# Hybrid decoder on one core: the two softmax maps of the prompt's attention are combined by ScalarE and GpSimd

## What is computed

```
s = jnp.einsum('bqhmd,bkhmd->bhmqk', qs, ks).astype(F32) * (DIFF_DH ** -0.5)
s = s + bias[None, :, None]
s = jnp.where(rel >= 0, s, jnp.finfo(F32).min)
p = jax.nn.softmax(s, axis=-1)
a = p[:, :, 0] - lam * p[:, :, 1]
return jnp.einsum('bhqk,bkhd->bqhd', a, v.astype(F32))
```

## Time and profile before

| What | Value |
|---|---|
| three runs, median (range) | 4095.96 us (4091.81 to 4100.94) |
| the profiled execution: its span | 4093.1 us; no time around it is listed |
| busy over the span: TensorE, VectorE, ScalarE, GpSimd | 90%, 45%, 28%, 3% |
| the prompt's attention, stretch 2322 to 3188 us | 866 us, 21% of the span |
| busy in that stretch: TensorE, VectorE, ScalarE, GpSimd | 757.94, 735.26, 571.56, 0 us |
| granted TensorE clock in that stretch | 0.96 of full speed |

### The profile page before, as it was taken

One profiled execution on the slowest core, in us unless ns is written; L12 is line 12 of the kernel. 1 busy time (PEld: TensorE's weight loads), 2 busy tenths in 40 slices (PEclk: granted clock), 3 DMA queues, 4 the chain that ended last, 5 costly groups with the idle time before them and its releaser, 6 DMA issues. The chain is left out here.

```text
span 4093.1 us, 57158 instructions
## 1 busy us (share of the span) xinstructions
PE 3702.2 (90%) x19551; PEld 3035.2 (74%) x19551; DVE 1841.7 (45%) x4144; ACT 1162.0 (28%) x1916; POOL 119.0 (3%) x156
## 2 busy tenths in 40 slices
PE   5999897995999989998999688888889799869999
PEld 4888796773888868887888577777777667458887
DVE  2222211555555531113222388888888222165554
ACT  2111111332222120102111266666666211121111
POOL 0000001110000000000000000000000000000000
PEclk9999998997999989999999899999999899879999
DMA  4211322336222231213212622222210546242221
GB/s 143 72 67 67 112 89 85 114 112 223 79 74 87 72 131 67 72 69 144 74 64 69 133 57 51 53 64 64 64 33 12 199 170 219 97 173 72 86 82 49
DMA packets 305344, 385.23 MB, mean 94 GB/s; under 512 B 153574, under 2 KB 211719, under 8 KB 305175
## 3 DMA queue, kind: packets, MB, share of 16 engines
q1 hardware_dynamic: 305174, 383.18, 28.9%
HBM read 278.63 MB, written 104.47 MB: 94 GB/s over the span
## 5 line engine op out<-in xcount | busy, mean ns | idle before, releaser
L234 PE MATMUL vg_ps_y<-vg_w_hi,vg_x_hi 128*128 128x512 f32 x1088 | 428.0, 393 | 10.9 <-ACT vg_w_hi L263 10.9
L236 PE MATMUL vg_ps_y<-vg_w_lo,vg_x_hi 128*128 128x512 f32 x1088 | 425.0, 391 | 0.0
L238 PE MATMUL vg_ps_y<-vg_w_hi,vg_x_lo 128*128 128x512 f32 x1088 | 424.8, 390 | 0.0
L1506 PE MATMUL att_ps_o<-att_v,att_a_t 128*128 128x128 f32 x2176 | 296.1, 285 | 51.0 <-ACT att_a_t L1567 50.6
L1506 PEld LDWEIGHTS att_ps_o<-att_v,att_a_t 128*128 128x128 f32 x2176 | 278.0, 197 | 76.0 <-ACT att_a_t L1567 53.2
L1634 DVE TENSOR_SCALAR_CACHE_REDUCE att_s<-att_ps_s,att_far 128x512 f32<-128x512 f32 (+3 forms) x608 | 326.6, 582 | 6.0 <-PE att_ps_s L1479 1.9
L1555 ACT ACTIVATE att_s<-att_s,att_neg 128x128 f32<-128x128 f32 (+15 forms) x256 | 307.2, 1200 | 2.7 <-DVE att_neg L1651 2.1
L1478 PE MATMUL att_ps_s<-att_k_hi,att_q_hl 128*128 128x512 f32 (+3 forms) x640 | 260.8, 414 | 11.7 <-DVE att_s L1634 10.8
L234 PEld LDWEIGHTS vg_ps_y<-vg_w_hi,vg_x_hi 128*128 128x128 f32 x1088 | 205.3, 189 | 53.3 <-issue 11.7
L238 PEld LDWEIGHTS vg_ps_y<-vg_w_hi,vg_x_lo 128*128 128x128 f32 x1088 | 205.2, 189 | 43.0
L236 PEld LDWEIGHTS vg_ps_y<-vg_w_lo,vg_x_hi 128*128 128x128 f32 x1088 | 205.3, 189 | 41.6
(11 more groups left out here) (269 smaller groups left out, 6431.2 us busy)
## 6 DMA issues: line engine op xcount, KB each, us to landing
smp_k_pg<-in_cache_k SPq DMA_DIRECT2D x64, 512.0 KB, 5.1
smp_v_pg<-in_cache_v SPq DMA_DIRECT2D x64, 512.0 KB
factors<-vg_out SPq DMA_DIRECT2D x68, 256.0 KB, 2.0
res_factors<-factors SPq DMA_DIRECT2D x34, 512.0 KB
res_o<-mixer_out SPq DMA_DIRECT2D x34, 512.0 KB, 4.4
att_k_nat<-out_k SPq DMA_DIRECT2D x128, 128.0 KB, 2.7
att_q_nat<-diff_q SPq DMA_DIRECT2D x128, 128.0 KB, 3.0
gla_x<-gla_qka SPq DMA_DIRECT2D x17, 520.0 KB, 3.4
```

Source lines behind the costliest of these rows:

```text
L234: nc.tensor.matmul(ps_y[g][:, 0:width[g]], x_hi[u][:, k, :], w_hi[:, k, cols], start=(k == 0), stop=False)
L236: nc.tensor.matmul(ps_y[g][:, 0:width[g]], x_hi[u][:, k, :], w_lo[:, k, cols], start=False, stop=False)
L238: mm = nc.tensor.matmul(ps_y[g][:, 0:width[g]], x_lo[u][:, k, :], w_hi[:, k, cols], start=False, stop=(k == KD - 1))
L1506: mm = nc.tensor.matmul(ps_o[:, 0:D_VD], a_t[n % 2][:, (b % 4) * P:(b % 4 + 1) * P], v_sb[u][:, b, :], start=(b == 0), stop=(b == i))
```

## The change

The pass over n columns leaves VectorE. The weight now has two buffers. ScalarE gets a new step `scale`, which multiplies the second map's exponentials in place by w, behind `high` and ahead of the next tile's `exps`. GpSimd gets a program for the phase: for each tile it waits for `p2_scaled` and for the buffer `a` to be turned, adds the two maps into `a`, and signals `a_done`. VectorE's `combine` ends with the weight.

```diff
-        weight = sb("weight", [P, 1])
+        weight = [sb(f"weight{i}", [P, 1]) for i in range(2)]
...
+                def scale(H, i):
+                    n = (i + 1) * P
+                    act.wait_ge(s["weight_done"], after(T * H + i + 1))
+                    nc.scalar.activation(s_sb[i % 2][:, 1, 0:n], s_sb[i % 2][:, 1, 0:n], ACT.Copy,
+                                         scale=weight[i % 2][:, 0:1]).then_inc(s["p2_scaled"], 1)
...
                             high(H + 1, 1 - u, slots(i)[1] + n, is_q, m, g)
                         more = not (last and i + 1 >= T)
+                        scale(H, i)
                         if more:
                             exps(*ahead(H, u, i, 1), 0)
...
-                    nc.vector.scalar_tensor_tensor(weight[:, :], total[i % 2][:, 0:1], core.neg_lambda[:, :],
+                    if not (isinstance(H, int) and H == 0 and i < 2):
+
+                        dve.wait_ge(s["p2_scaled"], after(T * H + i - 1))
+                    nc.vector.scalar_tensor_tensor(weight[i % 2][:, :], total[i % 2][:, 0:1], core.neg_lambda[:, :],
                                                    inv[i % 2][:, 1:2], ALU.mult, ALU.mult).then_inc(s["weight_done"], 1)
-                    dve.wait_ge(s["weight_done"], after(T * H + i + 1))
-
-                    dve.wait_ge(s["a_turned"], after(GROUPS * H + first_group[max(i - 1, 0)]))
-                    nc.vector.scalar_tensor_tensor(a[i % 2][:, 0:n], s_sb[i % 2][:, 1, 0:n], weight[:, :],
-                                                   s_sb[i % 2][:, 0, 0:n], ALU.mult, ALU.add).then_inc(s["a_done"], 1)
...
+            @block.gpsimd
+            def _(pool):
+                def head(H, u, last):
+                    for i in range(T):
+                        n = (i + 1) * P
+                        pool.wait_ge(s["p2_scaled"], after(T * H + i + 1))
+                        stand_alone(pool, core)
+
+                        pool.wait_ge(s["a_turned"], after(GROUPS * H + first_group[max(i - 1, 0)]))
+                        nc.gpsimd.tensor_tensor(a[i % 2][:, 0:n], s_sb[i % 2][:, 1, 0:n], s_sb[i % 2][:, 0, 0:n],
+                                                ALU.add).then_inc(s["a_done"], 1)
+
+                over_heads(pool, head)
```

More of the change, by code:

```diff
@@ L59, in __init__ @@
         self.passed = {e.engine: nc.alloc_semaphore(name=f"passed_{i}")
-                       for i, e in enumerate((nc.vector, nc.tensor, nc.sync))}
+                       for i, e in enumerate((nc.vector, nc.tensor, nc.sync, nc.gpsimd))}
     def sem(self, name):
@@ L1371, in attention @@
              ("turned hi_done lo_done piece_ready piece_free max_done neg_done exp_done inv_done "
-              "weight_done a_done a_turned a_copied a_met o_copied").split()}
+              "weight_done p2_scaled a_done a_turned a_copied a_met o_copied").split()}
         nat_in = [core.sem(f"att_nat_in{g}") for g in range(4)]
@@ L1653, in combine @@
                 def combine(H, u, i):
-                    n = (i + 1) * P
                     dve.wait_ge(s["exp_done"], after(2 * (T * H + i + 1)))
```

## The result

The changed kernel takes 4555.73 us (median of 4 runs, 4552.53 to 4558.17) against 4096.62 in the runs of the kernel before that were made beside it: ratio 1.112, interval 1.111 to 1.114, 459 us slower. The forecast was 4459 us, 363 slower, with a range of 4320 to 4650.

A forecast was written before the change was run, and what follows sets the result against it. TensorE and VectorE were taken as both nearly full in the phase. Stretch 635, scale 150, add 332, handovers 32 and clock 80 made 1229 us against 866, 363 more, hence 4459 us; range 4320 to 4650.

The forecast's parts named there:

- The ring: Attention phase: add, then turning, products, output or VectorE's take and weight, then scale, add, without overlap; 1229 us against 866.
- VectorE's side: VectorE's work between one add and the next scale, take and weight included; 523 us with handovers.
- The rival in which VectorE's relief makes the kernel faster: VectorE was the bound; scale and add hide beside TensorE, 108 us less, 3988 us; chance 0.03.
- stretch from add to scale, without the clock: Time from one add's end to the next scale, over 128 tiles: 635 us, ends 583 and 725.
- the clock: TensorE idles during scale and add, so its clock drops to the lower level: 80 us, ends 0 and 190.
- scale: ScalarE's new multiplication by the weight, 128 times: 150 us, ends 138 and 153.
- add: GpSimd's add of the two maps at 2.295 ns a column plus 0.1 us fixed: 332 us, ends 287 and 347.
- handovers: Weight to scale, scale to add, add to readers, some 0.25 us a tile: 32 us, ends 15 and 50.
- about 3.3 us of S run at the lower level: Tiles 8 to 15: part of the add-to-scale stretch at the lower clock, lengthening TensorE's side by 1.65 us, 1.1 taken.
- the rival of 190 us: Clock down through the whole add-to-scale stretch in large tiles: 190 us instead of 80, 4569 us; chance 0.2.
- three handovers a tile of some 0.1 us: Handovers on VectorE's side of the add-to-scale stretch, over 128 tiles: 38 us.
- small amounts at tiles 12 and 13: Excess of TensorE's and ScalarE's side over VectorE's in the add-to-scale stretch at these tiles: 0.8 us a head.

The follow-up runs named there:

- the scale's new place: Changed kernel with the next tile's scale moved ahead of the output and conversion in ScalarE's list; 4431 us, 1.083 of before.
- the run with half the fills: Changed kernel with useless matmuls on TensorE while it waits for GpSimd's add, 153 a head, none ahead of tile 5; 4417 us, 1.079 of before.
- the run with the shared last group: Kernel before, but in tiles 7 to 15 ScalarE scales and GpSimd adds the last column group beside VectorE's pass; 4100.4 us, 1.0016.
- 306 fills a head: Changed kernel with useless 128 x 128 matmuls on TensorE during its wait for the add in tiles 3 to 15, the full count; 4562 us.

## Why the prediction was right, and where it was off

**The mechanism: right.** The ring was forecast from the order of ScalarE's list and from the waits of `turn` and `take` on the add. The timeline shows each link, and the add on VectorE and the scale's new place bring back 180 and 125 us. As the forecast had it, VectorE's side is the larger part of the stretch and ScalarE's lateness is added to it. The rival in which VectorE's relief makes the kernel faster is out by the measured time, and the groups show why: VectorE spends what it was relieved of, and more, in waits for the add (340 and 85 us).

**The sizes.** The 127 rings of the changed kernel sum to 1312.6 us, against 1229 in the forecast:

| term | forecast | measured |
|---|---|---|
| stretch from add to scale, without the clock | 635 | 684 (the run with half the fills) |
| the clock | 80 | 131 (814.5 - 683.7) |
| scale | 150 | 153 |
| add | 332 | 317 |
| handovers | 32 | 28 (scale to add alone) |

Two terms were mis-sized, by 51 and 49 us, and carry the 84 us by which the rings are longer than forecast. (The phase is 17 us longer than its rings, which the sum left out; the kernel is 96 us over the forecast's difference.)

The first is the clock. The step was "about 3.3 us of S run at the lower level" with VectorE's side hiding a third. The trace shows 6.8 us at the lower level in a large tile, all but 0.9 of them in S: in tile 14 the stretch takes 10.0 us on average, and 8.0 with the fills, so the clock costs 2.0 us there and not 1.1. VectorE hides little, as its own pieces wait for TensorE's: 57 us of waits of `take` for scores, 1.9 before, and its side of the stretches falls from 638 to 562 us when the clock is up. The measured term lies about halfway to the rival of 190 us, which was offered at 0.2. The Trainium skill's rule (TensorE: Matmul & The Clock Gate, section "HAM oscillation — how this bites in real kernels"), an engine that waits in each step and starts each step slow, is what the traces show: 4.66 us without work, then 0.51.

The second is the stretch itself. With the clock up, VectorE's work in it is 494 us, where 485 were forecast, and its handovers are 40 us, where "three handovers a tile of some 0.1 us" came to 38. What failed is "small amounts at tiles 12 and 13", 0.8 us a head: ScalarE begins the scale later than the weight in all of tiles 1 to 13, mostly right behind the conversion `high`, and this sums to 50 us, 6.3 a head. The large amounts were right at tile 14 (8.0 us, forecast 7.9), too long at tile 15 (7.1, forecast 8.8) and too short at tile 0 (8.0, forecast 7.1). VectorE also waits 26 us for exponentials, which the forecast cost at nothing; it does so ahead of the weights of tiles 15 and 0, where ScalarE comes to the scale later still, so it lengthens nothing in these stretches.

Two of the recorded ends are added up wrongly: half of 112 off 635 is 579, not 583, and 88 on top is 723, not 725. The range doesn't change by it.

**The add.** It takes 2.10 ns a column and 0.19 us (from 458 ns at 128 and 4494 at 2048 columns), where I took 2.295 and 0.1. The faster of the two rows at 512 columns had about the right slope, the slower the right length at its size (1265 ns). The Trainium skill's figure of 4497 ns at 2048 columns (GPSIMD Engine Reference, section "3.1 Elementwise — side-by-side cycle accounting") agrees with the 4494 measured. Scaled by columns alone it gave 306 us, 11 too little, as it leaves out most of the fixed part of the shorter adds.

**Not tried.** GpSimd doing the weighted sum alone, with no scale; a third score buffer, which would take `take` out of the ring; and the weight ahead of the next tile's `take` in VectorE's list. For the last, the timeline above shows room: the exponentials of tile 14 are done at 3462.47, but its reciprocal stands behind all of tile 15's `take` and starts at 3466.30. What any of these would give stays open.

## What to carry to other kernels

Ask of a moved step where it stands in its new engine's list and what the row ahead of it waits for: a short row behind a wait for the end of the last tile starts late in every tile. Ask the same of the engine that the step has left: what stands behind it in the list, here `take`, used to follow at once and now waits for two other engines, because the buffers are only two. That turns a pipeline into a ring, in which every microsecond counts, on whichever engine; moving the late row up brought back only 125 us of 459 here. Two engines that are 88% and 85% busy say little of what relieving one is worth; the timeline of one tile, with who starts how long before whom, says more. Where a new wait lets TensorE idle in each step, price the clock with it: here it was over a quarter of the loss.

## What was not expected of the hardware

GpSimd's add all but stands still while VectorE runs a pass with two operands in SBUF: 1312 ns for 128 columns instead of 458, ending 0.32 us after the pass, while VectorE's passes kept their length (1285 ns at 1024 columns, as in the kernel before). The prediction had no place for it; it came up as a theory of the run with the shared last group. The Trainium skill states this in SBUF — State Buffer, section "Who interferes with whom": a VectorE instruction with two SBUF inputs and a GpSimd instruction that reads SBUF exclude each other, and the later one waits; the runs agree. In the changed kernel there is no sign of it: VectorE has no such pass left there, and the adds grow evenly from 458 to 4494 ns. And a plain float32 matmul as written ran as two: 306 fills a head were written and 4896 ran in eight heads.
